# Feed-forward down projection of a hybrid decoder layer: two half-sums of full products against seven block products per chunk

## What is computed

```python
h2 = rms_norm(x, norm2_g[l])
x = x + (jax.nn.silu(h2 @ w_ffn_gate[l]) * (h2 @ w_ffn_up[l])) @ w_ffn_down[l]
```

## Time and profile before

| what | value |
|---|---|
| median of 3 runs (lowest, highest) | 2110.78 us (2109.98, 2111.59) |
| the profiled execution, its span | 2111.37 us, 2109.7 us |
| mean granted clock of PE | 0.993 of full speed |
| PE, PEld busy | 97%, 79% of the span |
| DVE, ACT, POOL busy | 59%, 33%, 37% |
| one chunk of the feed-forward | 60.02 us (start of a chunk's first product to that of the next) |

### The profile page before, as it was taken

The page is one execution under the profiler, slowest core; times in us unless marked ns, Lnnn a source line. Parts: engine busy times, 40 slices in busy tenths (PEclk is TensorE's granted clock), DMA queues, the critical chain, the costliest instruction groups (busy, mean ns, idle before and its releaser), DMA issues. The chain is left out here.

```text
span 2109.7 us, 29366 instructions
## 1 busy us (share of the span) xinstructions
PE 2050.8 (97%) x9905; PEld 1674.3 (79%) x9905; DVE 1241.0 (59%) x1974; ACT 688.3 (33%) x1228; POOL 783.4 (37%) x697
## 2 busy tenths in 40 slices
PE   6999999999999999999998999988999999999999
PEld 5888888887777777777776888876888888888887
DVE  5768687743567766766756645567444444444544
ACT  4424333311334434434445100036223233322222
POOL 4413232322212211221220434358555555555552
PEclk9999999999999999999998999998999999999999
DMA  4112021223342243144354522211111111110112
GB/s 129 45 31 60 25 55 41 59 66 98 77 110 63 66 109 73 56 109 80 49 150 147 214 68 89 80 59 52 32 59 60 60 60 60 43 57 32 48 60 80
DMA packets 137744, 153.42 MB, mean 73 GB/s; under 512 B 7704, under 2 KB 112160, under 8 KB 137696
## 3 DMA queue, kind: packets, MB, share of 16 engines
q1 hardware_dynamic: 135952, 149.64, 25.8%
q10 hardware_dynamic: 1744, 3.15, 0.4%
HBM read 106.64 MB, written 20.97 MB: 60 GB/s over the span
## 5 line engine op out<-in xcount | busy, mean ns | idle before, releaser
L125 POOL TENSOR_TENSOR w_hi<-w_raw,w_ones 128x64 fp32r<-128x64 f32 x88 | 32.9, 374 | 1005.3 <-PE sb_g L151 464.1
L129 POOL TENSOR_TENSOR w_lo<-w_raw,w_hi 128x512 fp32r<-128x512 f32 x176 | 242.4, 1398 | 7.3
L813 DVE TENSOR_TENSOR sb_wt_lo<-sb_t,sb_wt_hi 128x512 fp32r<-128x512 f32 (+2 forms) x186 | 103.0, 554 | 113.2 <-ACT sb_wt_hi L634 111.3
L151 PE MATMUL sb_g<-h_hi,w_hi 128*128 128x512 f32 x544 | 153.0, 409 | 2.7 <-DVEq L693 1.9
L151 PE MATMUL sb_g<-h_lo,w_hi 128*128 128x512 f32 x544 | 150.6, 401 | 0.0
L151 PE MATMUL sb_g<-h_hi,w_lo 128*128 128x512 f32 x544 | 150.3, 400 | 0.0
L634 ACT CAST sb_wt_hi<-sb_t 128x512 fp32r<-128x512 f32 (+2 forms) x186 | 89.7, 482 | 166.6 <-PE sb_t L500 166.0
L2076 POOL TENSOR_TENSOR ff_w_lo<-raw_g,ff_w_hi 128x512 fp32r<-128x512 f32 x66 | 85.6, 1297 | 109.5 <-ACT ff_w_hi L2192 109.5
L151 PE MATMUL gla_g<-h_hi,w_hi 128*128 128x512 f32 x464 | 124.0, 402 | 0.0
L151 PE MATMUL gla_g<-h_lo,w_hi 128*128 128x512 f32 x464 | 122.8, 397 | 0.0
L151 PE MATMUL gla_g<-h_hi,w_lo 128*128 128x512 f32 x464 | 122.5, 397 | 0.0
(11 more groups left out here) (406 smaller groups left out, 4948.5 us busy)
## 6 DMA issues: line engine op xcount, KB each, us to landing
w_raw<-w_in SPq DMA_DIRECT2D x64, 512.0 KB, 8.1
raw_g<-w_ffn_gate SPq DMA_DIRECT2D x11, 1024.0 KB, 5.2
ff_raw_u<-w_ffn_up SPq DMA_DIRECT2D x11, 1024.0 KB, 5.7
ff_raw_d<-w_ffn_down SPq DMA_DIRECT2D x11, 1024.0 KB, 4.7
sb_qs<-sb_q_st SPq DMA_DIRECT2D x32, 256.0 KB, 5.1
sb_kh<-sb_k_st SPq DMA_DIRECT2D x32, 256.0 KB, 5.0
sb_kl<-sb_k_st SPq DMA_DIRECT2D x32, 256.0 KB, 5.0
mp_sig<-gates_t SPq DMA_DIRECT2D x16, 512.0 KB, 4.2
```

Source lines behind the costliest of these rows:

```text
L125: self.nc.gpsimd.tensor_tensor(hi[:, 0:64], raw[:, 0:64], self.ones[:], ALU.mult)
L129: ins = self.nc.gpsimd.tensor_tensor(lo[:, at], raw[:, at], hi[:, at], ALU.subtract)
L151: ins = nc.tensor.matmul(acc, a[:, k, :], b[:, k, half * HALF:(half + 1) * HALF], start=(n == 0), stop=(n == len(steps) - 1))
L813: nc.vector.tensor_tensor(wt_lo[:, m % 2, a:HALF], weight_bank(m, last)[:, a:HALF], wt_hi[:, m % 2, a:HALF], ALU.subtract).then_inc(lo_rea ...
```

## The change

The down projection becomes a 2 by 2 by 2 block product as well: rows (two halves of 512), hidden columns (two of 128) and output columns (two of 512). Seven block products P1 to P7, in the order D_ORDER, take the place of the eight that the 16 groups amount to. Each product has NG = 4 groups (tiles of 128 rows) of 3 matmuls. The products are accumulated in two sets of four banks, DX (Y and E) and DY (X and A), and after each product DVE adds the bank of each group to one block of `y` (`D_BLOCK`). That makes 28 adds per chunk where there were 16.

The scheme wants sums of the hidden quarters (`y_sum_1`, `y_sum_2`, `y_sum_3` on DVE, `y_sum_4` on POOL), sums of the down weights (`down_sum`, four, on POOL in place in `raw_d`), and high and low parts of seven hidden operands (ACT seven `y_round`, DVE three `y_low_part`, POOL four `y_low_pool_part`). The low parts of hidden operands lie where the exact values were, so a low part may be written only after everything that reads the exact value: `y_low_part(P6)` on DVE waits for `y_sum_4` on POOL. The ring of weight slots shrinks from six to four to make room; the last down product's weights go over `raw_d`, so that the next load of `raw_d` waits for the whole down block. In `gate_up` POOL's `sums_1` move behind the two P1 low parts, and `sum_2` and `sum_4` behind those of P5.

```diff
-    RING = 6
+    RING = 4
-    ND = TT * NH
-    SLOTS_PER = NP + 4
+    NG = TT // 2
+    ND = 7 * NG
+    SLOTS_PER = NP + 7
+    D_ORDER = (P1, P5, P6, P3, P7, P2, P4)
...
-        down = [E[0], E[1], A[0], A[1]]
+        DX = [Y[0], Y[1], E[0], E[1]]
+        DY = [X[0], X[1], A[0], A[1]]
...
+        D_CHAIN = {P1: DX, P6: DX, P7: DX, P4: DX, P5: DY, P3: DY, P2: DY}
+        D_BLOCK = {P1: (0, 0), P2: (0, 0), P6: (0, 1), P3: (0, 1), P5: (1, 1), P7: (1, 1), P4: (1, 0)}
...
-                    sp.wait_ge(w_ready, d_first(ch) + 4)
+                    sp.wait_ge(d_done, ND * ch + ND)
                     load_down(ch * PAIR + PAIR)
...
+                def y_low_pool_part(p, ch):
+                    pool.wait_ge(y_high, 7 * ch + Y_HIGH[p])
+                    pool.wait_ge(y_summed_pool, ch + 1)
+                    nc.gpsimd.tensor_tensor(y_lo[p][:], y_raw[p], y_hi[p][:], ALU.subtract).then_inc(y_low_pool, 1)
...
+                def down_block(ch):
+                    y_round(P3, ch)
+                    y_round(P7, ch)
+                    act.wait_ge(d_done, ND * ch + NG)
+                    down_high(4, ch)
+                    y_round(P2, ch)
+                    act.wait_ge(d_done, ND * ch + 2 * NG)
+                    down_high(5, ch)
+                    y_round(P4, ch)
+                    down_high(6, ch)
...
                         if i == 12:
-                            y_round(2, ch)
                             sigmoid(3, ch)
-                        if i == 13:
-                            y_round(3, ch)
+                            y_round(P5, ch)
+                            y_round(P6, ch)
+                        if i + RING >= NP:
+                            down_high(i + RING - NP, ch)
+                        elif i >= made:
+                            high(slot(i + RING), i + RING, ch)
...
+                def y_low_part(p, ch):
+                    dve.wait_ge(y_high, 7 * ch + Y_HIGH[p])
+                    if p == P6:
+                        dve.wait_ge(y_summed_pool, ch + 1)
+                    tt(y_lo[p][:], y_raw[p], y_hi[p][:], ALU.subtract).then_inc(y_low, 1)
...
                 def down_block(ch):
                     dve.wait_ge(gu_done, NP * ch + NP)
                     dve.wait_ge(c_step, STEPS * ch + STEPS)
-                    tt(u[0][:], X[U][:], cg[1][:], ALU.mult).then_inc(y_ready, 1)
-                    add(0, ch)
-                    y_low_part(3, ch)
-                    for n in range(1, ND):
-                        add(n, ch)
+                    tt(u[3], X[U][:], cg[1][:], ALU.mult).then_inc(y_ready, 1)
+                    y_low_part(P5, ch)
+                    for j in range(7):
+                        for g in range(NG):
+                            add(j, g, ch)
+                        if j == 0:
+                            y_low_part(P6, ch)
...
                 def down_block(ch):
-                    for n, (nh, t) in enumerate(D_GROUPS):
-                        if n % 8 == 0:
-                            pe.wait_ge(w_ready, d_first(ch) + 2 * nh + 2)
-                        if n == 0:
-                            pe.wait_ge(y_low, 4 * ch + 3)
-                        if n == 4:
-                            pe.wait_ge(y_low, 4 * ch + 4)
-                        pe.wait_ge(d_free, ND * ch + n + 1)
-                        rows = slice(t % 4 * P, (t % 4 + 1) * P)
-                        for q in range(6):
-                            f, kind = q // 3, q % 3
-                            a = (y_hi, y_hi, y_lo)[kind][:, f, t // 4, rows]
-                            b = (w_hi, w_lo, w_hi)[kind][ring(2 * nh + f)][:].rearrange("p k c -> p (k c)")
-                            ins = nc.tensor.matmul(down[n % 4][:], a, b, start=(q == 0), stop=(q == 5))
-                        ins.then_inc(d_done, 1)
+                    for j, p in enumerate(D_ORDER):
+                        pe.wait_ge(w_ready, d_first(ch) + j + 1)
+                        if p in (P1, P5, P6):
+                            pe.wait_ge(y_low, 3 * ch + {P1: 1, P5: 2, P6: 3}[p])
+                        else:
+                            pe.wait_ge(y_low_pool, 4 * ch + {P3: 1, P7: 2, P2: 3, P4: 4}[p])
+                        if j == 0:
+                            pe.wait_ge(c_step, STEPS * ch + 7)
+                        if j == 1:
+                            pe.wait_ge(y_ready, 4 * ch + 4)
+                        hi, lo = [w.rearrange("p k c -> p (k c)") for w in down_slot(j)]
+                        start = p in (P1, P5, P2)
+                        for g in range(NG):
+                            rows = slice(g * P, (g + 1) * P)
+                            if j >= 2:
+                                pe.wait_ge(d_free, d_read(j - 2, g, ch))
+                            passes = ((y_hi[p], hi), (y_hi[p], lo), (y_lo[p], hi))
+                            for n, (part, w) in enumerate(passes):
+                                ins = nc.tensor.matmul(D_CHAIN[p][g][:], part[:, rows], w, start=(start and n == 0),
+                                                       stop=(n == 2), skip_group_check=not start)
+                            ins.then_inc(d_done, 1)
```

More of the change, by code:

```diff
@@ L2123, in first_gate_up @@
                     for m in (G, U):
[L2124 removed]
+                        low(m, m, P5, 5 + m)
                     norm(2)
@@ L2134, in first_gate_up, with down_low, down_sum, y_sum_4 @@
                                 low((2 * n + m) % RING, m, p, 2 * n + m + 1)
[L2136 to L2140, removed]
+                def down_low(j, ch):
+                    pool.wait_ge(w_high, d_first(ch) + j + 1)
+                    hi, lo = down_slot(j)
+                    nc.gpsimd.tensor_tensor(lo, down_operand(j), hi, ALU.subtract).then_inc(w_ready, 1)
+                def down_sum(n, ch, lows, dst, left, right):
+                    pool.wait_ge(w_ready, d_first(ch) + lows)
+                    need(pool, b_made, 4 * ch + n if n else 0)
+                    nc.gpsimd.tensor_tensor(dst, left, right, ALU.subtract).then_inc(b_made, 1)
+                def y_sum_4(ch):
+                    pool.wait_ge(y_ready, 4 * ch + 4)
+                    pool.wait_ge(y_summed, 3 * ch + 3)
+                    nc.gpsimd.tensor_tensor(y_sum[P3], u[3], y_sum[P6], ALU.subtract).then_inc(y_summed_pool, 1)
+                def y_low_pool_part(p, ch):
[3 more added lines that the diff above has]
+                def down_block(ch):
+                    (b11, b12), (b21, b22) = b
+                    down_low(0, ch)
+                    down_sum(0, ch, 1, b11, b12, b11)
+                    down_sum(1, ch, 1, b12, b22, b12)
+                    down_low(1, ch)
+                    down_sum(2, ch, 2, b11, b22, b11)
+                    down_low(2, ch)
+                    y_sum_4(ch)
+                    down_low(3, ch)
+                    y_low_pool_part(P3, ch)
+                    down_sum(3, ch, 3, b11, b21, b11)
+                    down_low(4, ch)
+                    y_low_pool_part(P7, ch)
+                    down_low(5, ch)
+                    y_low_pool_part(P2, ch)
+                    down_low(6, ch)
+                    y_low_pool_part(P4, ch)
                 def norm_low(pair):
@@ L2151, in _ @@
                 with pool.Fori(0, N - 1, 1) as ch:
-                    down_low(ch)
-                    gate_up(ch + 1, lambda n: ring(4 + n), first(ch) + SLOTS_PER)
-                down_low(N - 1)
+                    down_block(ch)
+                    gate_up(ch + 1, lambda n: n % RING, first(ch) + SLOTS_PER)
+                down_block(N - 1)
             @block.scalar
```

183 lines of the change are left out of this document (111 added, 72 removed).

## The result

The changed kernel takes 2115.16 us (median of 20 runs, 2113.07 to 2117.55) against 2111.06 (20 runs, 2109.04 to 2113.16) on the same chip: ratio 1.0018, 95% interval 1.0011 to 1.0024. That is 3.8 us more, small but clear of no change by its interval, and inside the forecast's own range (2103 to 2118). Its profiled execution took 2114.52 us with a span of 2112.5.

What follows compares the result with a forecast made beforehand. PE, busy 97% of the span, bounds the kernel; waits (2.4 us) and new starts (0.3) eat the 2.72 saved: 0.0 a chunk, +0.5 at the end, 2111.3 us. Forecast 2103 to 2118; 8 in 10 runs 2094 to 2126.

Steps and rivals of the forecast that it cites:

- What goes: Down block: 96 matmuls become 84, 2.72 us less in each of 11 chunks, 29.9 us if PE never waits.
- the schedule: One chunk's instructions timed from the earlier trace's rows; the down block ends at 27.4 us, as before.
- The conflict: DVE with two SBUF inputs and POOL shut each other out; in turns, 1.69 us a pair against 0.73 alone.
- the tie: Down block: POOL's `down_low(2)` ready at 8.72 us, level with DVE's low part for P5 (from 8.71).
- PE's waits: Down block, each chunk: PE waits 1.1 us for P5's low part and 1.3 us for P6's.
- A new start: PE restarting after a wait in the down block: 0.15 us each, 0.3 a chunk.
- The sum of a chunk: Full chunk: 2.4 us of waits and 0.3 of new starts eat the 2.72; change 0.0.
- this branch: If POOL goes first at the tie: one PE wait of 2.2 us in place of two, same end.
- End of the program: Last 16 output transfers run at their limit in 10.9 us; the last lands 0 to 1 us later, counted 0.5.
- What is late behind: POOL's line to the next chunk's third product: `low(2)` ready at 32.4 us, wanted at 32.8, fits by 0.4.
- time 0: The schedule's origin within a chunk: the end of product 12.
- The rival of a further turn lost: At P6's low part or before the third product: 1.15 to 1.24 us a chunk slower, 2124.5 us; chance 0.19.

Runs made afterwards that it cites:

- Experiment 1: Changed kernel without POOL's four sums of down weights, output not the layer's: 2096.7 us, ratio 0.9934 to the kernel before.
- experiment 2: Changed kernel without `y_sum_1` and `y_sum_2` on DVE, output not the layer's: 2095.16 us, ratio 0.9925 to the kernel before.
- experiment 3: Changed kernel with P6's low part in a place of its own, so it needn't wait for `y_sum_4`: 2116.4 us, ratio 1.0025.
- experiment 4: Changed kernel with POOL making the P2 low parts ahead of `sums_1` in gate_up: 2116.44 us, ratio 1.0023.
- 5: Changed kernel with the edits of experiment 3 and experiment 4 together: 2111.04 us, ratio 1.0001.
- experiment 7: 5 with DVE's and ACT's turns reordered, three of POOL's four down-weight sums made early, and POOL's down block reordered: 2094.59 us, ratio 0.992.
- 9: experiment 7 with POOL's order changed: `y_sum_4` ahead of `down_low(3)`, P3's low part ahead of `down_low(4)`: 2095.38 us, ratio 0.9925.

## Why the prediction was right, and where it was off

- **What goes.** 2.72 us of PE's work a chunk went. The extra 0.17 in the first group, which the earlier trace rows shows and the schedule kept, went too: P1 starts with no gap (1784.29 in the views above) and ended at 8.16, not 8.33. A term of -0.17 was missing. The prediction took the 0.17 for a cost of each loop pass. It was PE waiting for a low part: in the earlier trace rows DVE's low part, held up by POOL, ends at 1784.26 (1783.24 + 1.02), and PE's first matmul of the down block starts 0.13 later:

```profile
1784.39 0.49 PE L2477 MATMUL ff_e_g<-ff_w_hi,ff_y_hi 128*128 128x512 f32 x1
```

  The same 0.13 to 0.14 stands in the other chunks of the loop. P1's low part of the changed kernel is ready long before, so this wait isn't there.
- **The conflict.** Every turn of the schedule up to P6 came at its place: `y_sum_3` 0.70 (forecast 0.70), `y_sum_1` 5.81 (5.77), `y_sum_2` 7.52 (7.46), P5's low part 9.44 (9.40), P6's 13.64 (13.58). Experiment 1 shows that it is the conflict and not DVE's own work, and the rows of 1.6 us and more show it instruction by instruction; experiment 2 agrees by 0.74 us. What the Trainium skill (SBUF — State Buffer, "Who interferes with whom") says of two exclusive users is borne out at every pair shown, and so is its remark that the order of issue decides who blocks: at the tie DVE's instruction began at 1787.61 and POOL's at 1787.62, and DVE took 0.68 and POOL 1.82.
- **PE's waits.** From the end of a product to the release by the low part: 9.44 - 8.16 = 1.28 for P5 and 13.64 - 12.58 = 1.06 for P6, against 1.1 and 1.3.
- **A new start.** This is the term that was mis-sized: 0.15 counted, 0.42 measured. From P5's low part (9.44) to the end of its product (12.58) are 3.14 us, and 12 matmuls take 2.72. 0.14 lies between DVE's end and the first matmul (1788.29 to 1788.43). The other 0.28 is in the first group of three, as the chain shows behind P6's wait: 0.96 in place of 0.68. Of that, 0.10 is the second matmul's later start (1788.43 to 1788.76, where 0.23 is usual). Most of the rest comes from how the wait is counted, from the end that the profile gives the matmul before it: rows are 0.39 long but start 0.23 apart, so 0.16 of each is hidden while matmuls follow each other. Counted from start to start, PE loses 1.58 + 0.10 = 1.7 us at P5, the same as 1.28 + 0.42.

```profile
1792.62 0.96 PE ff_y_g L2591 x3
1793.57 0.69 PE ff_y_u L2591 x3
```

  The rows of the kernel before held this price. From the low part's end at 1784.26 to the end of the first group, 1784.51 + 1.53 = 1786.04, are 1.78 us, and 6 matmuls take 1.36: 0.42. The prediction read only the group's own excess, 1.53 against 1.36, and missed the part of the start that the running product 14 had hidden.
- **The sum of a chunk.** 1.28 + 1.06 + 2 x 0.42 - 2.72 - 0.17 = +0.29, and 60.30 - 60.02 = 0.28. The forecast was 0.0. Ten chunks make 2.8 us.
- **The last chunk.** There the tie went the other way, by 0.07 us: POOL's instruction began at 2089.11 and DVE's at 2089.18.

```profile
2089.11 1.26 POOL L2176 TENSOR_TENSOR ff_w_lo<-ff_raw_d,ff_w_hi 128x512 fp32r<-128x512 f32 x1 [1.80 <-ACT ff_w_hi L2273]
```

```profile
2089.18 1.75 DVE L2417 TENSOR_TENSOR ff_u_lo<-ff_u,ff_y_hi 128x512 fp32r<-128x512 f32 x1
```

```profile
2091.02 0.47 PE L2591 MATMUL ff_x_g<-ff_w_hi,ff_y_hi 128*128 128x512 f32 x1 [2.53 <-DVE ff_u_lo L2417]
...
2092.62 0.63 PE L2591 MATMUL ff_x_u<-ff_w_hi,ff_u_lo 128*128 128x512 f32 x1
2093.04 0.63 PE L2591 MATMUL ff_a_g<-ff_w_hi,ff_y_hi 128*128 128x512 f32 x1
```

  The prediction had this branch, one long wait with the same end. It wasn't the same end: after 2.53 us of waiting the matmuls stood 0.43 apart, the lower clock level (granted 0.53 of full speed from 2091.80 to 2095.40), and P5's product took 4.42 us where it should take 2.72. In ten chunks of eleven the waits, 1.48 at most, left the clock alone (granted 1.00), as forecast. But a wait of 2.5 us doesn't always bring the clock down. The eleventh chunk of experiments 3, 4 and 5 has the same wait of 2.52 us. In 4 the clock fell as well (0.52). In 3 and 5 it stayed at 1.00, and P6's first matmul started 2.99 us after P5's, not 4.42; here is 3:

```profile
2092.71 0.47 PE L2591 MATMUL ff_x_g<-ff_w_hi,ff_y_hi 128*128 128x512 f32 x1 [2.52 <-DVE ff_u_lo L2417]
...
2095.70 0.47 PE L2591 MATMUL ff_y_g<-ff_w_hi,ff_y_hi 128*128 128x512 f32 x1
```

  The last down block, from its first matmul to its last one's end, is 23.6 us (2085.62 to 2109.21) against 22.0 before (2084.45 to 2106.49): 1.5 us more. Where the clock stayed up, in 3 and 5, it is 22.3 and 22.2. So the branch has the same end as long as the clock holds. What decides that is open, and so is why DVE comes later only in the last chunk (there its multiplication L2492 begins 0.78 us after L2478, in the loop 0.72).
- **Luck.** In the loop DVE was 0.01 us ahead in the chunk shown, and the ten waits of 1.40 to 1.48 say that it was first in all ten; the schedule called it a tie. Had POOL won there, each chunk would have had the wait of 2.5 us, and up to 1.4 us more whenever the clock fell (23.6 against 22.2): an estimate of up to 14 us over ten chunks, beyond the forecast's range.
- **End of the program.** 3.3 us from the last matmul's end to the end of the span, 3.2 before: 0.1, not 0.5. Ten chunks, the last one and the end make 4.4 us, where the interval of the ratio says 2.3 to 5.1. The two spans differ by 2.8, since in the one of after the last down block began only 1.2 us later and not 2.8: what lies ahead of it varies by that much from execution to execution (the second chunk begins at 1506.18 before, at 1504.82 after, and at 1501.75 to 1506.75 in the runs of the experiments). In the faster kernels the end takes longer: 5.6 us in experiment 7 (2088.28 to 2093.9), 5.2 in 9. In 7, DVE's adds are about 2 us behind PE when the first output leaves and end 1.56 us after PE does (0.72 in the changed kernel). They come every 0.60 us, faster than the outputs leave at some 380 GB/s, so that the span ends 4.1 us after the last add, 2.6 in the changed kernel, whose outputs leave at the same rate but whose adds come only every 0.68 us. These 2.3 us are most of the reason why 7 wins 20.6 us and not the 11 x 2.13 = 23.4 that its period says.
- **What is late behind.** POOL's `low(2)` began at 1810.13 and ended 32.6 us after time 0 (1811.42 - 1778.85), forecast 32.4; PE wanted it at 1811.95 (its first matmul starts at 1811.78 in the timeline). The sentence that PE can't be 0.4 us a chunk quicker if only its own waits were shorter is what experiment 3 then showed. The rival of a further turn lost didn't come in the changed kernel. Nor did it in experiment 3, where POOL lost as many turns as before and its room at the third product was used up by PE coming sooner.

What stays open: what makes the clock fall or hold after the same wait of 2.5 us, and whether any order at all gives 57.1. A ring of four slots by itself wasn't tried.

## What to carry to other kernels

Before moving work to an engine with idle time, lay its instructions and those of the engine it shares a path with side by side in order of time, and price each meeting by a pair of rows; here shares of 46% and 65% hid 2.6 us of waiting a chunk. Then look for gaps in which the new work meets nobody: three instructions moved forward were worth 17 us, more than all reordering at the crowded place. Count for each wait of PE its new start as well, and expect that removing one wait shows the next, so read the queue behind it before promising the whole gain.

## What the runs showed of the hardware

- A wait of PE on another engine costs more than its length: 0.42 us here (0.14 to the first matmul, 0.28 in the first group of three, 0.16 of it by the way the wait is counted), for waits of 1.06 and 1.28 us. It was the same 0.42 in the kernel before, where the release came while PE's product 14 was still ending and the profile listed no wait.
- PE's clock: ten waits of 1.40 to 1.48 us left it at 2.4 GHz. The wait of 2.5 us stands in the last chunk of four traces: in two (the changed kernel and experiment 4) the level of 1.2 GHz came 0.8 and 1.0 us after the restart, in the changed kernel for some 3.5 us at 1.7 us of time; in two (experiments 3 and 5) the clock stayed at 2.4 GHz. The earlier trace rows has 1.83 harmless and 3.58 not.
- At a near-tie between DVE (two operands in SBUF) and POOL, 0.01 us of lead decided in the chunk shown, and 0.07 us the other way in the last. The loser pays 1.07 (DVE) or 0.53 (POOL).
